# A decoder block on one core: the matmuls on zeros before the first products are left out

## The chip, the cores and the metric

The kernel runs on one core of a Trainium2 chip. The metric is the time of one execution on the device in microseconds (us). One execution was also recorded by the profiler; every row below comes from it, and its times count from the start of its span.

## The reference

One layer of a hybrid decoder on x (1 x 1024 x 1024, float32). Two parts, each with an RMSNorm before and after and a residual:

```python
h = rms_norm(x, norm_mix_pre)
proj = h @ w_in                       # 1024 x 1792
u_pool, g_b, g_c, u_conv, q, k, v = split(proj)
y_pool = pool_mixer(u_pool, pool_w, pool_scale)
y_conv = g_b * causal_dwconv(g_c * u_conv, conv_w)
y_attn = swa_sink_attention(q, k, v, attn_sinks)
x = x + rms_norm(concat(y_pool, y_conv, y_attn) @ w_o, norm_mix_post)
h = rms_norm(x, norm_ffn_pre)
up = causal_dwconv(h @ ffn_w_up, ffn_conv_w) + ffn_conv_b     # 1024 x 5632
x = x + rms_norm((silu(gate) * val) @ ffn_w_down, norm_ffn_post)
```

## The kernel before

The program is written by hand for each engine, in order, with semaphores between them. Rows of x are normalised in 8 tiles of 128 tokens, turned with TensorE transposes so that channels stand on the partitions, and multiplied by the weights. Each float32 operand is split into a rounded high part (ScalarE, into a float32r tile) and the low rest (VectorE), and a product is three matmuls: high by high, high by low, low by high (`product`, L1613 to L1619). After the projection come attention, pooling and convolution, the output projection, the up projection and the down projection, the last two partly with seven products in place of eight. TensorE works through all of it in the order in which its block of the program is written.

The change lies at the start of that block. What is before it on each engine:

- SyncE (L548 to L562) starts the loads in this order: x tiles 0 and 1, the identity matrix, the gain as 8 rows, weight tile 0, x tiles 2 and 3, and so on.
- GpSimd sets small constants (L642 to L644), among them `pool_mat`, a 128 x 256 tile of zeros that is later filled with the pooling weights; the semaphore `set_` counts these. Then it makes the mean square and its root for each tile (`root`, L645).
- ScalarE squares tiles 0 and 1 (`square_x`, L757), rounds weight tile 0 (L744), rounds turned tiles 0 and 1 into `hhi` (`round_h`, L768), and squares tiles 2 and 3.
- VectorE normalises tiles 0 and 1 (`norm_x`, L1126), copies the turned gain (L1161), multiplies the turned tiles 0 and 1 by it in PSUM (`scale_turned`, L1155), makes the low part of weight tile 0 (L1116) and of x tiles 0 and 1 (`low_h`, L1138), and then normalises tiles 2 and 3 (L1131).
- TensorE waits until the constants are set, runs 8 matmuls of `pool_mat` with itself into bank 0 of PSUM (`keep_clock(8)`), waits for the identity and the gain rows, turns the gain (L1684), turns x tiles 0 and 1 (`turn_x`, 8 transposes each, L1626), and runs 4 more matmuls on zeros (`keep_clock(4)`). Their result is read by nobody: the first product into the same bank starts its accumulation anew. A call of a 128 x 256 float32 matmul is two records in the trace.

Then the projection begins, by pairs of x tiles. For the first pair weight tiles 0 and 1 are multiplied in three passes of 8 matmuls each (`channels_by_pass`, L1645, matmuls at L1664) so that a pass can start when its operand is there. For weight tile 0 the passes are high by high (A), weight's low part (B), x's low part (C). In weight tile 1 the turn of x tile 2 stands before the first pass and that of tile 3 before the second. From the second pair on the three matmuls of a product follow each other (L1616 to L1618), and the turns of the tiles 4 to 7 come between the weight tiles.

Of the kernel before, what the change touches and what calls it, by code (L numbers as in the profile page):

```python
# [24 lines left out]
P = 128  # L25
# [55 lines left out]
def build(nc, consts, x, norm_mix_pre, w_in, pool_w, pool_scale, conv_w, attn_sinks, w_o,  # L81
# [18 lines left out]
    with ctx:  # L100
        def alloc(stack, name, shape, dt=F32):
            return stack.enter_context(nc.sbuf_tensor(name, shape, dt))
# [69 lines left out]
        pool_mat = alloc(xb_, "pool_mat", [P, 2, P])  # L172
# [55 lines left out]
        ps = ctx.enter_context(nc.psum_tensor("ps", [P, 8, HALF], F32))  # L228
# [1383 lines left out]
        def _(pe):  # L1612
# [17 lines left out]
            def turn_x(t):  # L1630
                if t >= 2:
                    pe.wait_ge(ht_split, t - 1)
                turn(t, hrow_a[:, t % 2, :])
# [37 lines left out]
            def project(m, n, c, ks=range(KD)):  # L1671
                return channels(use_banks(m) + c, n % SPLIT, hhi, hlo, half_of(c), ks)

            def keep_clock(n):

                for _ in range(n):
                    pe.matmul(ps[:, 0, 0:2 * P], pool_mat[:, 0, :], pool_mat[:, :, :],
                              start=True, stop=True)

            pe.wait_ge(set_, 3)  # L1680
            keep_clock(8)
            pe.wait_ge(ident_in, 16)
            pe.wait_ge(gain_rows_in, 16)
            pe.transpose(ps[:, 3, 0:KD], gain_rows[0:KD, :], ident[0:KD, 0:KD])              .then_inc(gain_turned, 1)  # L1684
            turn_x(0)
            turn_x(1)
            keep_clock(4)

            for pair in range(NT // 2):
                tiles = slice(2 * pair, 2 * pair + 2)  # L1690
# [104 lines left out]
            for u in range(SLOTS):  # L1795
                n, c = SLOT0 + u // 2, u % 2
# [202 lines left out]
```

## Time and profile before

| what | value |
| --- | --- |
| median of 3 runs | 950.22 us (950.14 to 950.29) |
| the profiled execution, its own time | 950.0 us |
| its span, first to last instruction | 948.2 us |
| TensorE busy, share of the span | 938.9 us, 99% |
| VectorE, ScalarE, GpSimd busy | 654.7, 433.5, 189.4 us |
| mean granted clock of TensorE | 0.999 |

Engines are PE (TensorE's matmuls), PEld (its weight loads, which overlap them), DVE (VectorE), ACT (ScalarE), POOL (GpSimd) and SP (SyncE). A transpose is a matmul of its line L1626. A record of a matmul is longer than the step to the next one, because matmuls are pipelined: the step is the rate, the record the latency. Where several instructions of one kind follow each other, a timeline prints one row with their count and the time from the first start to the last end.

### The profile page before, as it was taken

How to read it: one execution, taken by the hardware profiler on the slowest of the kernel's cores; microseconds unless marked ns; L12 is line 12 of the kernel's file. 1: busy time of each engine (PE TensorE's matmuls, PEld its weight loads, DVE VectorE, ACT ScalarE, POOL GpSimd, SP SyncE). 2: the span in 40 equal slices, each digit the busy share in tenths (PEclk: the TensorE clock that was granted, in tenths of full speed). 3: DMA queues.
4: the chain of work that ended last, by engine and by line, in shares of the span. 5: the costliest groups of instructions: out<-in, count | busy, mean ns of one | idle time of the engine just before them, and what ended most of it. 6: DMA issues, size and time to landing. Idle time of an engine off the chain costs nothing.

```text
span 948.2 us, 11487 instructions
## 1 busy us (share of the span) xinstructions
PE 938.9 (99%) x4419; PEld 777.9 (82%) x4419; DVE 654.7 (69%) x710; ACT 433.5 (46%) x648; POOL 189.4 (20%) x182
## 2 busy tenths in 40 slices
PE   8999999999999999999999999999999999999997
PEld 7988887887888888888888888888888888888886
DVE  6645795766655899777877787778776653535668
ACT  5524444444433555445443444444444454335353
POOL 3301000000111424242223333443431100000021
PEclk9999999999999999999999999999999999999999
DMA  6999971005322236486343446554647775677455
GB/s 225 269 328 231 209 145 45 23 23 178 134 89 89 90 97 206 142 184 183 115 141 100 145 112 133 112 143 105 140 91 208 201 235 214 228 267 264 163 171 200
DMA packets 114248, 151.16 MB, mean 159 GB/s; under 512 B 6289, under 2 KB 66193, under 8 KB 114193
## 3 DMA queue, kind: packets, MB, share of 16 engines
q1 hardware_dynamic: 100737, 118.63, 38.5%
q0 software_dynamic: 13456, 31.79, 16.8%
q8 instruction: 35, 0.57, 0.3%
q14 instruction: 20, 0.16, 0.1%
HBM read 113.17 MB, written 60.29 MB: 183 GB/s over the span
## 4 chain that ended last, share of the span: by engine, by line
PE 97%; DVE 1%; DMA 0%; ACT 0%; POOL 0%; issue 0%; DVEq 0%; POOLq 0%; SPq 0%; ACTq 0%
PE ps L1616 30%; PE ps L1618 30%; PE ps L1617 30%; PE ps L1626 1%; PE ps L1751 1%; PE ps L1774 1%; PE ps L1752 1%; PE ps L1760 1%; PE ps L1778 1%; DMA xin<-in_x 0%; DVE hlo L1138 0%; PE ps L1789 0%; DVE ps L1155 0%; PE ps L1664 0%; DVE x2b L1427 0%
## 5 line engine op out<-in xcount | busy, mean ns | idle before, releaser
L1616 PE MATMUL ps<-hhi,whi 128*128 128x512 f32 (+1 forms) x240 | 91.1, 379 | 0.5 <-DVE hlo L1138 0.5
L1618 PE MATMUL ps<-hhi,wlo 128*128 128x512 f32 (+1 forms) x240 | 88.5, 369 | 0.0
L1617 PE MATMUL ps<-hlo,whi 128*128 128x512 f32 (+1 forms) x240 | 88.5, 369 | 0.0
L686 POOL TENSOR_TENSOR w_sums<-wraw 128x1024 f32<-128x1024 f32 x20 | 48.4, 2421 | 185.8 <-DVE w2lo L1373 63.0
L648 POOL TENSOR_SCALAR meansq<-sumsq 128x1 f32<-128x1 f32 x28 | 10.0, 357 | 373.4 <-ACT yg L1042 170.8
L1616 PEld LDWEIGHTS ps<-hhi,whi 128*128 128x128 f32 x240 | 45.3, 189 | 8.0 <-DVE hlo L1138 0.7
L1001 ACT ACTIVATE yg<-ps,par_b 128x1024 f32<-128x1024 f32 x21 | 25.3, 1207 | 57.9 <-DVE ps L1499 57.9
L1618 PEld LDWEIGHTS ps<-hhi,wlo 128*128 128x128 f32 x240 | 45.2, 189 | 7.7
L1617 PEld LDWEIGHTS ps<-hlo,whi 128*128 128x128 f32 x240 | 45.3, 189 | 7.4 <-issue 0.5
L1447 DVE SCALAR_TENSOR_TENSOR yg<-ps,par_a,yg 128x1023 f32<-128x1023 f32 x22 | 28.2, 1282 | 26.9 <-ACT yg L1001 26.9
L1616 PE MATMUL ps<-h2hi,whi 128*128 128x512 f32 x116 | 45.4, 391 | 0.2 <-DVE wraw L1148 0.2
L1618 PE MATMUL ps<-h2hi,wlo 128*128 128x512 f32 x116 | 45.2, 389 | 0.0
L1617 PE MATMUL ps<-h2lo,whi 128*128 128x512 f32 x116 | 45.1, 389 | 0.0
L1461 DVE TENSOR_TENSOR w2lo<-wraw,w2hi 128x1024 fp32r<-128x1024 f32 x23 | 27.8, 1223 | 23.5 <-ACT w2hi L1031 23.1
L1616 PE MATMUL ps<-r_hi,whi 128*128 128x512 f32 x112 | 43.6, 389 | 0.0
L1618 PE MATMUL ps<-r_hi,wlo 128*128 128x512 f32 x112 | 43.6, 389 | 0.0
L1618 PE MATMUL ps<-r_hi,w2lo 128*128 128x512 f32 x112 | 43.6, 389 | 0.0
L1616 PE MATMUL ps<-r_hi,w2hi 128*128 128x512 f32 x112 | 43.6, 389 | 0.0
L1617 PE MATMUL ps<-r_lo,w2hi 128*128 128x512 f32 x112 | 43.6, 389 | 0.0
L1616 PE MATMUL ps<-r_hi,h2hi 128*128 128x512 f32 x112 | 43.6, 389 | 0.0
L1617 PE MATMUL ps<-r_lo,h2hi 128*128 128x512 f32 x112 | 43.6, 389 | 0.0
L1618 PE MATMUL ps<-r_hi,h2lo 128*128 128x512 f32 x112 | 43.6, 389 | 0.0
(261 smaller groups left out, 2709.1 us busy)
## 6 DMA issues: line engine op xcount, KB each, us to landing
wraw<-in_ffn_w_up SPq DMA_DIRECT2D x42, 512.0 KB, 5.2
s_dram<-in_ffn_w_down POOLq DMA_DIRECT2D x6, 2816.0 KB, 28.1
wraw<-r_dram SPq DMA_DIRECT2D x44, 256.0 KB, 3.7
wraw<-s_dram SPq DMA_DIRECT2D x44, 256.0 KB, 4.9
r_dram<-cst SPq DMA_DIRECT2D x33, 256.0 KB, 2.8
wraw<-act_dram SPq DMA_DIRECT2D x33, 256.0 KB, 3.6
wraw<-in_ffn_w_down SPq DMA_DIRECT2D x33, 256.0 KB, 4.6
wraw<-in_w_in SPq DMA_DIRECT2D x14, 512.0 KB, 10.2
```

Source lines behind the costliest of these rows:

```text
L648: pool.tensor_scalar(meansq[:, i:i + 1], sumsq[:, i:i + 1], 1.0 / DM, EPS, ALU.mult, ALU.add).then_inc(ms_ready, 1)
L686: pool.tensor_tensor(w_sums[:, 0:2, :], raw[:, 0:4:3, :], raw[:, 2:3, :].broadcast_to([P, 2, HALF]), ALU.add)\
L1001: act.activation(yg[:, pair % 2, :], banks(4 * (pair % 2)), ACT.Identity, bias=ffn_bias(pair), scale=ffn_tap(2, pair)).then_inc(yg_started, 1)
L1447: finish_step(dve.scalar_tensor_tensor(y[:, 1:], src[:, :SEQ - 1], ffn_tap(1, f), y[:, 1:], ALU.mult, ALU.add))
L1461: dve.tensor_tensor(lo, raw, hi, ALU.subtract).then_inc(d_split, 1)
L1616: pe.matmul(acc, w_hi, x_hi, start=first, stop=False, skip_group_check=looped)
L1617: pe.matmul(acc, w_hi, x_lo, start=False, stop=False, skip_group_check=looped)
L1618: return pe.matmul(acc, w_lo, x_hi, start=False, stop=last, skip_group_check=looped)
L1626: last = pe.transpose(ps[:, b + k // 4, (k % 4) * P:(k % 4 + 1) * P], rows[:, k * P:(k + 1) * P], ident)
L1751: pe.matmul(acc, q, k_hi[:, kv, keys], start=True, stop=False)
L1752: last = pe.matmul(acc, q, k_lo[:, kv, keys], start=False, stop=True)
L1760: last = pe.transpose(ps[:, 6, i * P:(i + 1) * P], s_sb[:, u % 2, i, :], ident)
```

## The change

The helper `keep_clock` and its two calls are taken out; nothing else differs.

```diff
-            def keep_clock(n):
-
-                for _ in range(n):
-                    pe.matmul(ps[:, 0, 0:2 * P], pool_mat[:, 0, :], pool_mat[:, :, :],
-                              start=True, stop=True)
-
             pe.wait_ge(set_, 3)
-            keep_clock(8)
             pe.wait_ge(ident_in, 16)
             pe.wait_ge(gain_rows_in, 16)
             pe.transpose(ps[:, 3, 0:KD], gain_rows[0:KD, :], ident[0:KD, 0:KD])              .then_inc(gain_turned, 1)
             turn_x(0)
             turn_x(1)
-            keep_clock(4)
```

## Rows read from the trace of the kernel before

**Rows 1.** The page: busy time of each engine; shares of the chain by engine.

```profile
PE 938.9 (99%) x4419; PEld 777.9 (82%) x4419; DVE 654.7 (69%) x710; ACT 433.5 (46%) x648; POOL 189.4 (20%) x182
...
PE 97%; DVE 1%; DMA 0%; ACT 0%; POOL 0%; issue 0%; DVEq 0%; POOLq 0%; SPq 0%; ACTq 0%
```

**Rows 2.** Busy by stretch (PE first, records started), then TensorE's waits after 60 us.

```profile
30.00:60.00 30.00, 30.00 (x190) 27.00 (x189) 17.20 (x18) 11.93 (x12) 7.12 (x13) 1.00 0.95 290
...
PE ps L1616 <- DVE wraw L1148: 0.2, 1, 0.2
```

**Rows 3.** Timeline of TensorE, 0 to 13 us: start, length, line, count, [idle before].

```profile
1.26 5.57 PE L1677 MATMUL ps<-pool_mat 128*128 128x256 f32 x16 [1.26 <-POOL pool_mat L644]
...
7.25 1.09 PE L1626 MATMUL ps<-cst,hrow_a 128*128 128x128 f32 x8 [0.27 <-DVE hrow_a L1126]
8.72 1.09 PE L1626 MATMUL ps<-cst,hrow_a 128*128 128x128 f32 x8 [0.38 <-DVE hrow_a L1126]
9.65 1.89 PE L1677 MATMUL ps<-pool_mat 128*128 128x256 f32 x8
12.24 0.98 PE L1664 MATMUL ps<-hhi,whi 128*128 128x256 f32 x6 [0.70 <-ACT hhi L768]
```

**Rows 4.** Line L1677 in four stretches: count, ns min/median/max, first and last start.

```profile
L1677 PEld LDWEIGHTS ps<-pool_mat x8: 287/337/337, 1.3 to 4.0; 128*128 128x128 f32 x8
L1677 PE MATMUL ps<-pool_mat x7: 634/634/794, 1.3 to 4.0; 128*128 128x256 f32 x7
...
L1677 PE MATMUL ps<-pool_mat x4: 380/558/634, 4.0 to 5.2; 128*128 128x256 f32 x4
...
L1677 PEld LDWEIGHTS ps<-pool_mat x8: 190/190/192, 9.5 to 10.9; 128*128 128x128 f32 x8
L1677 PE MATMUL ps<-pool_mat x8: 379/379/382, 9.6 to 11.2; 128*128 128x256 f32 x8
```

**Rows 5.** Line L1677 on PE by stretch: stretch, length, busy (records), granted clock, DMA.

```profile
1.26:4.40 3.14, 3.14 (x7) 1.00 0.84 284
```

**Rows 6.** The chain that ended last, 7.9 to 21.2 us: start, length, what.

```profile
7.91 0.49 DVE hrow_a L1126
...
8.77 2.36 DVE ps L1155 x2
...
12.26 2.28 DVE hlo L1138 x2
...
18.79 1.04 ACT hhi L768
...
21.14 0.39 PE ps L1616
```

**Rows 7.** Busy of the five engines in stretches at the end, then granted clock, DMA.

```profile
946.00:947.00 1.00, 0.00 (x0) 0.00 (x0) 0.00 (x0) 0.00 (x0) 0.00 (x0) 1.00 1.00 387
947.00:948.20 1.20, 0.00 (x0) 0.00 (x0) 0.00 (x0) 0.00 (x0) 0.00 (x0) 0.55 0.20 77
```

**Rows 8.** Lines L1626 and L1664: ns min/median/max, first and last start.

```profile
L1626 PE MATMUL ps<-cst,hrow_a x64: 272/273/330, 7.2 to 33.6; 128*128 128x128 f32 x64
...
L1664 PE MATMUL ps<-hhi,wlo x16: 279/283/283, 13.3 to 20.4; 128*128 128x256 f32 x16
```

**Rows 9.** Timeline of TensorE, 13 to 18 us.

```profile
13.29 1.12 PE L1664 MATMUL ps<-hhi,wlo 128*128 128x256 f32 x8
14.58 1.21 PE L1664 MATMUL ps<-hlo,whi 128*128 128x256 f32 x8 [0.17 <-DVE hlo L1138]
15.86 1.06 PE L1626 MATMUL ps<-cst,hrow_a 128*128 128x128 f32 x8
16.68 1.20 PE L1664 MATMUL ps<-hhi,whi 128*128 128x256 f32 x8
17.72 1.04 PE L1626 MATMUL ps<-cst,hrow_a 128*128 128x128 f32 x8
```

**Rows 10.** Timeline of VectorE, the normalising of tile 2.

```profile
14.44 1.27 DVE L1131 SCALAR_TENSOR_TENSOR hrow_a<-xin,rstd,gain_a 128x1024 f32<-128x1024 f32 x1
```

## The prediction

> **What bounds the kernel now.** I read the page's header parts first. TensorE is busy for 938.9 of 948.2 us, and of the chain that ended last 97% is TensorE [rows 1]. So a delay of TensorE reaches the end of the kernel unless a later wait swallows it. The second reading asks for such waits: from 30 to 60 us TensorE is busy for all 30.00 us, and after 60 us it waits once, for 0.2 us [rows 2]. There is no slack that could take up a delay. What is left is the first 21 us, where TensorE waits for others, and where the removed instructions lie.
>
> The timeline of TensorE there [rows 3] shows the first burst of matmuls on zeros from 1.26 to 6.83 us (8 calls, 16 records), the turn of the gain row, the turns of x tiles 0 and 1 at 7.25 and 8.72, the second burst from 9.65 to 11.54 (4 calls, 8 records), and the first useful product, pass A of weight tile 0, at 12.24. Neither burst holds anybody up: the turn at 7.25 waited for the normalised rows and pass A for the rounded ones; the table names VectorE and ScalarE as releasers.
>
> The rows that matter are those of the bursts themselves [rows 4]. A record that started up to 4.0 us takes 634 ns, its weight load 337 ns; from 5.2 us on and in the second burst it is 379 and 190 ns. The steps changed alike: seven starts in the 3.14 us from 1.26 give 0.449 us, while the second burst gives (1.89 - 0.379)/7 = 0.216 us, a factor of 2.08. [...] From the whole first burst: 5.57 - 0.38 = 5.19 us are 15 steps, n of them slow, n x 0.449 + (15 - n) x 0.216 = 5.19, so n = 8.4, and the change came 3.8 us after 1.26, at about 5.0 us; the mixed row from 4.0 to 5.2 fits. The granted-clock column prints 1.00 for 1.26 to 4.40 us all the same [rows 5], so I trust the durations and not that column.
>
> **What the change does.** It takes out 24 matmul records and adds no wait. Time taken off the path: none. Both bursts ended before what follows them could begin. The turn of the gain row may start earlier, since it stands behind the burst, but the copy that reads it stands on VectorE behind the normalising of tile 1, which the chain contains [rows 6]: worth 0.
>
> The second burst alone would also be worth about 0. It fills a pause that would last from 9.81 (end of the second turn) to 12.24, 2.4 us. At the end of the kernel TensorE issues its last product shortly before 942.6, and the granted clock is still 1.00 until 947.0 and 0.55 on average from there [rows 7], so it fell at about 947.1, after 4.5 us of idleness. A pause of 2.4 us should not lower it.
>
> The first burst is what counts. Without it TensorE does nothing for 6 us and starts the turns at the lower level. **Term 1, the turns.** Eight take 1.09 us now, with 0.273 us for one [rows 3, 8]: a step of (1.09 - 0.273)/7 = 0.117 us. No row shows a slow turn. The bounds on the factor are 337/190 = 1.77 (weight loads) and 2.08 (steps); I take 1.9, between them, since a turn is a short load and a short stream: 0.222 us. Tile 0 starts at 7.25 as now; tile 1 is in the queue behind it and starts at 7.25 + 8 x 0.222 = 9.03 (its rows are there at 8.66); its last turn starts at 10.58 and takes 0.273 x 634/379 = 0.46, so it ends at 11.04. VectorE now begins scaling tile 1 at 9.95, half-way through the pair of 2.36 us that starts at 8.77 [rows 6], held by its own queue and not by the turn. With a semaphore's 0.04 it begins at 11.08: **+1.13 us**. Tile 0's scaling (about 9.3 for 8.77) hides in that. All of the scaled path, rounding on ScalarE included, moves by 1.13, so pass A starts at 13.37.
>
> **Term 2, the passes.** Passes A and B of weight tile 0 are 16 matmuls. The step at full clock is (1.12 - 0.283)/7 = 0.12 us [rows 8, 9]; times 1.9 it is 0.228, and 16 of them last until 13.37 + 3.65 = 17.02. When does the clock rise? The only case in this trace is 3.8 us of unbroken work before the change; from 13.37 that is 17.17, just as pass C starts, of which one step stays slow (0.1 us). Pass C needs the low parts of x, ready at 14.54 + 1.13 = 15.67: no wait any more. C, turn 2, the first pass of weight tile 1 and then turn 3 follow: 8 x 0.12 + 0.10 = 1.06, then 0.82 and 1.04 (the differences of starts 15.86, 16.68, 17.72 [rows 9]): turn 3 starts at 19.94 in place of 17.72, **+2.2 us**. The two waits that TensorE has now in this stretch, 0.2 us before pass C and about 0.3 before turn 2 (its rows come at 14.44 + 1.27 = 15.71 [rows 10]), are swallowed. VectorE's rows for turns 2 and 3 come at 16.8 and 18.6, both earlier than TensorE gets there.
>
> From turn 3 on the chain is turn, rounding at 18.79, low part, first product of the next pair, 21.14 now [rows 6]: everything follows turn 3, so the lag of 2.2 stays, and there is no later slack.
>
> **Sum.** The traced execution took 950.0 us, span 948.2, and the median of the runs is 950.22. 950.0 + 2.2 = 952.2 for a profiled one, 952.4 against the median. With 1.77 for the factor the same working gives +1.8 (turns 0.9 of it); with 2.08, +2.6. A difference under 0.2%, 1.9 us, can't be told from none here, and the forecast stands a little beyond it.
>
> [...]
>
> **Rivals.**
> 1. *The turns themselves raise the clock.* Slow turns would run from 7.25 to 11.04 without a pause, 3.8 us, as long as the first burst needed. Then the pause to 13.37 (2.3 us, under the 4.5 of [rows 7]) keeps the clock up, passes run fast, and only term 1 is left: +1.1, 951.35, not slower by the bound. It decides if the rise comes before about 16.5 us, because each slow us of passes costs 0.47 us. For it: the near equality of the two times. Against it: the turns at 7.25 came when the clock was already up, so no row shows that turns raise it. [...] Chance 0.27, with rises inside passes A and B.
> 2. *The rise comes later than in the first burst.* 3.8 us is one observation. If pass C and turn 2 stay slow too, C ends at 17.02 + 1.82 = 18.84, turn 2 at 20.6, and turn 3 starts at 21.7: +3.9 to +4.0, 954.2; half-way there, 953.3. Nothing in the rows excludes it. Chance 0.25.
> 3. *The clock stays low up to the next pair.* TensorE turns between passes would break up the work. C, turn 2, pass, turn 3 and two more passes at 1.8 us each from 17.02 end at 27.9, where the pair's products start now at 21.14 (+6.7), and their first 3.8 us cost 1.8 more: +8.5, 958.7. Against it: A, B and C are 5.5 slow us without a turn between. Chance 0.04.
> 4. *Nothing happens*: the clock is full from the start, as the column says [rows 5]: 950.2. Against it: 634 for 379 ns. With it, a gain, for which I find no place. Chance 0.04.
>
> **The numbers.** The forecast has 0.40, at 952.4, its own range 952.0 to 952.8. The range reaches down to rival 1 with term 1 at factor 1.77 (950.22 + 0.9 = 951.1) and up to rival 2's end with 0.1 to spare (954.3); outside are rivals 3 and 4 and a few in a hundred beside. Slower by over 0.2% (above 952.1) are nearly all of the forecast, 0.35 of 0.40, and rivals 2 and 3: 0.64 in all, of which I keep 0.62. Within 0.2% are rival 1, the lowest forecasts and rival 4: 0.36. Faster 0.02.
>
> **What would show it.** In the changed trace: transposes of tiles 0 and 1 with longer records (about 0.46 us) and a step of 0.22; scaling of tile 1 near 11.1; pass A at 13.4 with records near 0.47 and a step of 0.23, falling to 0.283 and 0.12 near 17.2; turn 3 near 19.9 and the first product of pair 1 at 23.3; from there every start later by the same 2.2. Records of pass A at 0.283 mean rival 1; of pass C and turn 2 at the slow length, rival 2. The prediction is wrong if turns are fast from the beginning, or if the lag at 60 us isn't the lag at the end.

## The result, and the profile after

| | before | after |
| --- | --- | --- |
| median | 950.26 us | 952.15 us |
| lowest to highest, 16 runs each | 949.96 to 950.44 | 951.32 to 953.26 |
| the profiled execution, span | 950.0, 948.2 us | 951.97, 950.2 us |

The ratio is 1.0022, with an interval of 1.0015 to 1.0029: 1.9 us slower, where 2.2 had been forecast. The second row of the table is as telling as the first. The kernel before repeats within 0.5 us, the changed one spreads over 1.9 us, and its times gather near 952.0 (10 of 16 between 951.86 and 952.29) and near 953.1 (5 of 16 between 953.03 and 953.26); one is at 951.32. Beside the experiments below single times of the kernel before lie between 949.66 and 951.15, so only a spread well beyond that says something.

First the page of the changed kernel, for the rows that answer to [rows 1], then two of TensorE's waits (us in total, how often, the longest).

```profile
PE 934.0 (98%) x4395; PEld 775.0 (82%) x4395; DVE 654.9 (69%) x710; ACT 433.5 (46%) x648; POOL 189.6 (20%) x182
...
PE 97%; DVE 1%; ACT 1%; DMA 0%; POOL 0%; issue 0%; DVEq 0%; POOLq 0%; ACTq 0%
```

```profile
PE ps L1664 <- ACT hhi L768: 2.4, 1, 2.4
...
PE ps L1616 <- DVE wraw L1148: 0.2, 1, 0.2
```

24 records are gone, and TensorE is busy for 4.9 us less in a run that is 2 us longer. (Lines after the removed helper have moved; L1677 is here the turn of the gain row.) The last of these waits is the only one after 30 us, as in [rows 2]: no slack has appeared. The pause before pass A, where the second burst stood, is 2.4 us. The two short waits of [rows 3, 9] before pass C and turn 2 have gone.

The timeline of TensorE, against [rows 3, 9]:

```profile
6.23 0.24 PE L1677 MATMUL ps<-cst,gain_rows 8*128 8x8 f32 x1 [6.23 <-DMA cst<-consts_dram]
7.58 3.68 PE L1626 MATMUL ps<-cst,hrow_a 128*128 128x128 f32 x16 [1.11 <-DVE hrow_a L1126]
13.64 2.08 PE L1664 MATMUL ps<-hhi,whi 128*128 128x256 f32 x8 [2.38 <-ACT hhi L768]
15.52 1.56 PE L1664 MATMUL ps<-hhi,wlo 128*128 128x256 f32 x8
16.91 1.12 PE L1664 MATMUL ps<-hlo,whi 128*128 128x256 f32 x8
...
19.70 1.04 PE L1626 MATMUL ps<-cst,hrow_a 128*128 128x128 f32 x8
```

And the records of the two lines, by stretch, against [rows 8] (count, ns min/median/max):

```profile
L1626 PE MATMUL ps<-cst,hrow_a x16: 421/421/476, 7.6 to 10.8; 128*128 128x128 f32 x16
...
L1664 PE MATMUL ps<-hhi,whi x8: 415/415/580, 13.6 to 15.3; 128*128 128x256 f32 x8
...
L1664 PE MATMUL ps<-hlo,whi x8: 278/283/288, 16.9 to 17.7; 128*128 128x256 f32 x8
```

The turns (421 ns a record, 273 in [rows 8]) and pass A (415 ns) run at the lower level from end to end, pass B changes in its middle, pass C (283 ns) is at the higher one. As the first burst did [rows 4], TensorE's first work begins slow: here these are the turns, after 6.23 us with nothing to do, the 8 x 8 turn of the gain and a pause of 1.11. Steps: (3.68 - 0.42)/15 = 0.217 us for turns, and between the starts of A and B 1.88/8 = 0.235. B to C is 1.39 = n x 0.235 + (8 - n) x 0.12, where n is the number of steps still at the lower level; so n = 3.7, and the clock rose at 15.52 + 0.87 = 16.4 us.

The chain in this stretch, against [rows 6]:

```profile
7.58 3.69 PE ps L1626 x16
...
11.30 1.24 DVE ps L1155
...
12.56 1.03 ACT hhi L768
...
13.64 4.39 PE ps L1664 x24
```

Before, VectorE stood in this chain from 8.77 to 14.54, one operation behind the other, and TensorE only came in with pass C. Now the chain goes through both turns, once over VectorE and ScalarE, and then stays on TensorE. This is how a slower engine takes over a chain that it had not been on.

The column of the granted clock (the number after the five engines) shows nothing of the slow turns, as it showed nothing in [rows 5]:

```profile
7.00:11.20 4.20, 3.62 (x16) 3.28 (x16) 2.59 (x4) 1.40 (x3) 0.97 (x2) 1.00 0.95 300
```

So the 1.97 us by which this execution is behind the traced one of before are: 0.33 because its first turn began at 7.58 and not at 7.25 (the rows of x came later: VectorE began on them at 6.77 us, 6.44 before; nothing in the edit touches these loads, and in all 14 traces, with and without the bursts, it begins between 6.19 and 6.84); 1.07 for the turns (pass A begins 6.06 us after the first turn, before 4.99); 0.58 for the passes (turn 3 begins 6.06 us after pass A, before 5.48). Against the median of before, 950.26, this execution is 1.7 us behind: the traced one of before was itself a short one.

### The profile page after: what moved, and what is told of

It is laid out like the page before. It is cut to its first block, busy times and chain, and to the rows that moved or that the text cites. A ratio compares the mean times of both kernels' runs of the same rounds, so it can differ in the third digit from the quotient of the medians.

```text
span 950.2 us, 11439 instructions
## 1 busy us (share of the span) xinstructions
PE 934.0 (98%) x4395; PEld 775.0 (82%) x4395; DVE 654.9 (69%) x710; ACT 433.5 (46%) x648; POOL 189.6 (20%) x182
## 4 chain that ended last, share of the span: by engine, by line
PE 97%; DVE 1%; ACT 1%; DMA 0%; POOL 0%; issue 0%; DVEq 0%; POOLq 0%; ACTq 0%
PE ps L1616 30%; PE ps L1618 30%; PE ps L1617 30%; PE ps L1626 2%; PE ps L1743 1%; PE ps L1766 1%; PE ps L1744 1%; PE ps L1752 1%; PE ps L1770 1%; PE ps L1664 1%; DMA xin<-in_x 0%; PE ps L1781 0%; ACT hhi L768 0%; DVE x2b L1427 0%; DVE ps L1155 0%; DVE hlo L1138 0%
## 5 line engine op out<-in xcount | busy, mean ns | idle before, releaser
L1617 PE MATMUL ps<-r_lo,whi 128*128 128x512 f32 x112 | 43.6, 389 | 0.0
```

Source lines behind the costliest of these rows:

```text
L1617: pe.matmul(acc, w_hi, x_lo, start=False, stop=False, skip_group_check=looped)
```

## The experiments

Three questions stood open. Is the loss made of the two terms? Do turns raise the clock? And what is each burst worth? The medians below are of 11 runs each. Every edit shown below is against the kernel before.

| run | median, lowest to highest | ratio to before, interval |
| --- | --- | --- |
| again (the changed kernel) | 952.04, 951.12 to 953.18 | 1.0018, 1.0009 to 1.0027 |
| fill_matmuls | 951.22, 951.08 to 951.55 | 1.0010, 1.0001 to 1.0019 |
| fill_turns | 951.28, 950.94 to 951.37 | 1.0010, 1.0002 to 1.0019 |
| second_only | 951.25, 951.19 to 951.40 | 1.0011, 1.0002 to 1.0019 |
| first_only | 951.02, 950.29 to 952.30 | 1.0009, 1.0001 to 1.0018 |
| first_six | 950.90, 950.07 to 952.06 | 1.0006, 0.9997 to 1.0015 |
| first_half | 951.90, 951.25 to 952.77 | 1.0018, 1.0010 to 1.0027 |
| late_start | 951.55, 951.17 to 951.79 | 1.0013, 1.0004 to 1.0021 |
| second_1 | 950.26, 950.09 to 951.26 | 1.0003, 0.9994 to 1.0012 |
| second_2 | 950.21, 949.91 to 951.19 | 1.0001, 0.9992 to 1.0010 |

The kernel before had 950.22, 950.27 and 950.25 beside them.

### The changed kernel again

No edit in any of the three.

> The changed kernel once more, beside the experiments of this call, to see whether its time and the moment at which the clock rises repeat. My theory (the start at the lower clock costs about 1.1 us in the turns of x tiles 0 and 1 and about 0.9 us in the passes of weight tile 0, and all of it reaches the end): median 952.0 to 952.5. In the first profile the records of pass B shortened at about 16.4 us, 2.8 us after pass A began. Rival A (the moment is always the same distance behind the work): again 2.8 us, single times within 0.3 us of each other. Rival B (the moment moves from execution to execution): another distance here, and single times spread over more than 1 us, as they did (951.3 to 953.3).

> A third look at the changed kernel, to see which moments of the clock come with which time. Two looks so far: rise at 16.4 us (951.97), and rise at 9.9, fall at 13.7, rise at 17.1 (951.4). Theory (the loss is 0.45 to 0.5 us for each slow us in which passes or turns on the chain run, whatever the moments): the sum from this look's own records agrees with its time within 0.3 us. For a time near 953.2 the rise should come at 18.5 us or later.

> A fourth look at the changed kernel, for the same reading as the third: the start of turn 3 behind that of the kernel before, against the time behind 950.2, should agree within 0.3 us, and slow records in passes A to C or in turn 2 should account for all of it beyond 1.0 us.

The first had 11 runs, the other two one execution each (953.83 and 953.02 us). In the profile of the first (951.40 us) the timeline of TensorE reads:

```profile
6.99 3.43 PE L1626 MATMUL ps<-cst,hrow_a 128*128 128x128 f32 x16 [0.60 <-DVE hrow_a L1126]
12.80 1.57 PE L1664 MATMUL ps<-hhi,whi 128*128 128x256 f32 x8 [2.38 <-ACT hhi L768]
14.17 1.91 PE L1664 MATMUL ps<-hhi,wlo 128*128 128x256 f32 x8
```

and its busy time by stretch (stretch, length, busy time and records, granted clock, then what the DMA moved):

```profile
12.80:13.60 0.80, 0.80 (x6) 0.91 1.18 357
13.60:16.40 2.80, 2.80 (x15) 0.50 0.46 172
16.40:17.40 1.00, 1.00 (x9) 0.77 0.01 4
```

The last turns are already fast (3.43 in place of 3.68), pass A starts fast, and then the clock falls. A mean of 0.91 over 0.8 us, where the column prints 0.50 while the clock is down, means half the clock for 0.14 us of it, so the fall was at 13.46, with TensorE at work for 0.7 us after its pause of 2.4; 0.77 over 1 us puts the rise at 16.86. In the other two every turn of tiles 0 and 1 is at the lower level (3.68 us). In again_c (953.02 us) it is low to the beginning of turn 2:

```profile
13.47 2.07 PE L1664 MATMUL ps<-hhi,whi 128*128 128x256 f32 x8 [2.38 <-ACT hhi L768]
15.34 1.91 PE L1664 MATMUL ps<-hhi,wlo 128*128 128x256 f32 x8
17.05 1.91 PE L1664 MATMUL ps<-hlo,whi 128*128 128x256 f32 x8
18.75 1.23 PE L1626 MATMUL ps<-cst,hrow_a 128*128 128x128 f32 x8
```

Three passes of 1.91 us, and a turn that is slow in its first part (1.23 for 1.03). again_b has the same picture and 953.83 us, 0.8 more, which lies in its first turn: it began at 8.22, because the gain row, which stands before it in TensorE's queue, landed only at 8.0. Rival B holds: the same work behind the same pause sees the clock rise at 16.4, at 9.9 with a fall at 13.46, or in the course of turn 2, at about 19 (again_c) and 20 (again_b). Behind the start of pass A that is 2.8, 5.7 and 5.8 us where it had not risen before.

Both expectations on the sum hold as well. The start of turn 3 and the execution's own time, each behind the traced execution of before (17.72 and 950.0):

| profile | first turn | pass A | turn 3 | behind at turn 3 | own time | behind at the end |
| --- | --- | --- | --- | --- | --- | --- |
| before | 7.25 | 12.24 | 17.72 | | 950.00 | |
| changed | 7.58 | 13.64 | 19.70 | 1.98 | 951.97 | 1.97 |
| again | 6.99 | 12.80 | 19.09 | 1.37 | 951.40 | 1.40 |
| again_b | 8.22 | 14.28 | 21.62 | 3.90 | 953.83 | 3.83 |
| again_c | 7.41 | 13.47 | 20.77 | 3.05 | 953.02 | 3.02 |
| fill_matmuls | 7.53 | 13.58 | 19.05 | 1.33 | 951.37 | 1.37 |
| fill_turns | 7.45 | 13.50 | 18.98 | 1.26 | 951.29 | 1.29 |
| first_only | 7.58 | 12.46 | 18.76 | 1.04 | 951.02 | 1.02 |
| late_start | 7.65 | 14.61 | 19.50 | 1.78 | 951.73 | 1.73 |
| first_half | 7.34 | 13.16 | 20.24 | 2.52 | 952.50 | 2.50 |
| second_only | 7.34 | 13.40 | 18.88 | 1.16 | 951.19 | 1.19 |
| first_six | 7.62 | 12.62 | 18.93 | 1.21 | 951.17 | 1.17 |
| second_1 | 7.96 | 12.65 | 18.96 | 1.24 | 951.26 | 1.26 |
| second_2 | 7.53 | 12.53 | 18.14 | 0.42 | 950.43 | 0.43 |

Nothing after turn 3 takes up or adds more than 0.07 us, in any of these 14 profiles.

### The two terms apart: the pause filled

```diff
-            keep_clock(8)
...
-            keep_clock(4)
+            keep_clock(2)
```

> No first burst; 2 calls on zeros (4 records) after the turns of x tiles 0 and 1, which fill the pause before pass A: 4 x 0.449 = 1.8 us from about 11.0, so they end before pass A at 13.4. The turns stay at the lower clock: +1.1 stays. My theory (unbroken work raises the clock, and here it is unbroken from 7.3 us on): the clock rises before pass A or early in it, and term 2 is gone: 951.3 to 951.6. Rival (only the work of pass A and after it counts, or the moment is a matter of chance): as the changed kernel, 952.2.

```diff
-            keep_clock(8)
...
-            keep_clock(4)
+            for _ in range(9):
+                pe.transpose(ps[:, 0, 0:P], pool_mat[:, 0, :], ident)
```

> As the run with 2 calls on zeros, but the pause is filled with 9 turns of zeros (9 x 0.222 = 2.0 us), so that TensorE does nothing but transposes from 7.3 to about 13.3 us. If turns raise the clock as matmuls do: records shorten before or early in pass A, 951.3 to 951.6, like the run with matmuls. [...]

```diff
-            keep_clock(8)
...
             keep_clock(4)
```

> No first burst, the second of 4 calls (8 records) stays. After slow turns that end at about 11 us, 8 records at the lower clock take 8 x 0.449 = 3.6 us, so the burst, if the clock doesn't rise in it, ends at about 14.5 and holds pass A back by 1.1 us. My theory: the clock rises within or at the end of the burst, the passes run fast, pass A starts between 13.4 and 14.5, waits before pass C and turn 2 take up some of it: 951.4 to 952.1. Rival (the clock rises no sooner than in the changed kernel): pass A late and slow, 953.

All three give 951.2 to 951.3, and all 33 times lie between 950.94 and 951.55. In each, pass A begins 6.05 or 6.06 us after the first turn, as in the changed kernel, and turn 3 5.47 or 5.48 us after pass A, as in the kernel before. That is term 1 alone, measured: +1.0 us (1.06 from first turn to pass A in the profiles). The rivals, 952.2 for fill_matmuls and 953 for second_only, are out; the two fills came a shade under the 951.3 to 951.6 expected. Term 2 is the rest, 952.1 - 951.25 = 0.9 us on average, and it is what spreads. second_only came out below the 951.4 to 952.1 expected, because the clock rose within its 8 records: the burst took 2.77 us and didn't hold pass A back.

The timeline of fill_turns, and below it the records of its 9 added turns and of the matmuls that follow:

```profile
7.45 3.68 PE L1626 MATMUL ps<-cst,hrow_a 128*128 128x128 f32 x16 [1.14 <-DVE hrow_a L1126]
10.91 2.13 PE L1687 MATMUL ps<-cst,pool_mat 128*128 128x128 f32 x9
13.50 1.21 PE L1664 MATMUL ps<-hhi,whi 128*128 128x256 f32 x8 [0.46 <-ACT hhi L768]
```

```profile
L1687 PE MATMUL ps<-cst,pool_mat x9: 421/421/421, 10.9 to 12.6; 128*128 128x128 f32 x9
...
L1664 PE MATMUL ps<-hhi,whi x8: 278/282/387, 13.5 to 14.4; 128*128 128x256 f32 x8
```

TensorE did nothing but transposes from 7.45 to 13.04, all of them at the lower level, and the matmuls after them run at the higher one (the longest, 387 ns, is the first after a pause: in the changed kernel that one took 580). So turns do raise the clock. In the profile of again, too, the records of turns shortened at about 9.9 us with only turns (and the 8 x 8 turn of the gain) before them.

### What the second burst is worth

```diff
             keep_clock(8)
...
-            keep_clock(4)
```

> The first burst of 8 calls back in, the second burst of 4 left out. My theory: the pause between the turns and pass A is 2.4 us, too short to lower the clock, so the second burst is worth nothing: 950.2 +- 0.2, turns with records of 0.273 us, pass A at about 12.24 with records of 0.283. Rival (the second burst holds the clock through the pause): pass A and part of B at records of 0.415 us, turn 3 about 1 us later, 951.2.

I was wrong here. The rival holds in its numbers, though the fall came within pass A and not ahead of it. The median is 0.8 us above the kernel before and single times spread over 2 us, from 950.29 to 952.30. The timeline:

```profile
1.26 6.24 PE L1677 MATMUL ps<-pool_mat 128*128 128x256 f32 x16 [1.26 <-POOL pool_mat L644]
...
12.46 1.48 PE L1664 MATMUL ps<-hhi,whi 128*128 128x256 f32 x8 [2.44 <-ACT hhi L768]
13.74 1.91 PE L1664 MATMUL ps<-hhi,wlo 128*128 128x256 f32 x8
15.45 1.65 PE L1664 MATMUL ps<-hlo,whi 128*128 128x256 f32 x8
```

and its stretches:

```profile
12.40:13.60 1.20, 1.14 (x8) 0.84 1.08 328
13.60:16.20 2.60, 2.60 (x14) 0.50 0.72 255
16.20:17.20 1.00, 1.00 (x9) 0.78 0.53 90
```

The clock was up for the turns (records of 273 ns), TensorE paused for 2.44 us, pass A began at full clock, and at 12.40 + 0.82 = 13.22 the clock fell and stayed down to 16.64. Pass A's first records alone would show nothing: the price of the pause came 0.8 us after it had ended, under dense work. That the pause brings it on rests on comparison: with 4 records put into it (second_2, fill_matmuls), 8 (the kernel before, second_only) or 9 turns (fill_turns) no profile has such a fall.

Two runs with a shorter pause, `keep_clock(4)` replaced by 2 calls and by 1:

> The kernel before with 2 calls in place of 4 in the second burst: TensorE stands still for about 1.6 us before pass A (0.7 in the kernel before, 2.4 without the burst). Without the burst single times spread from 950.3 to 952.3, and the profile showed the clock falling 1 us after pass A began. Theory P (a pause of 2.4 us can lower the clock, depending on where it falls; the second burst is there for that): something between, a median of 950.2 to 950.6, with a few times near 951. Rival (only the end of the first burst matters, the pause doesn't): as without the second burst, 951.0 with times up to 952.3.

> The same with 1 call: a pause of about 2.0 us. Theory P: median 950.3 to 951.0, spread of the single times nearer to 2 us. Rival: 951.0 with times up to 952.3, as without the burst.

Medians of 950.21 and 950.26, which can't be told from before. The spread hints at an effect that the medians hide. With 1 call (a pause of 2.2 us) 4 of 11 times are above 951.0; with 2 calls (1.6 us) one, at 951.19, and another at 950.89. Of the kernel before, 3 of 87 runs beside these experiments are above 951.0, but 2 of those are among the 21 that ran beside these two. Theory P fits, and is shown only weakly by these times; that 2 calls are worse than 4 isn't shown, and the median of 1 call is just below the 950.3 to 951.0 that it expected. The profile of second_1, 951.26 us, is one of its slow four:

```profile
12.65 1.21 PE L1664 MATMUL ps<-hhi,whi 128*128 128x256 f32 x8 [2.19 <-ACT hhi L768]
13.70 1.68 PE L1664 MATMUL ps<-hhi,wlo 128*128 128x256 f32 x8
```

```profile
13.60:14.60 1.00, 1.00 (x9) 0.70 1.15 373
```

Again fast at first (1.21 us for pass A), slow later. By its granted clock (0.70 over 1 us, so half the clock for 0.6) the fall came at 14.0, 1.35 us after pass A began. From pass A to turn 3 this execution needs 6.31 us, 0.83 more than before.

### What the length of the first burst is worth

The second burst left out in both, the first of 6 and of 4 calls.

> A first burst of 6 calls (12 records), no second burst: to about 5.8 us if the clock rises at 5.0. Theory 1 (the burst need only last until the clock rises): 950.2 with single times within 0.3 us. If the moment of the rise moves from execution to execution by more than a microsecond: most times at 950.2, some at 952.

> A first burst of 4 calls in place of 8, no second burst: 8 records from 1.26 to about 4.9 us, all at the lower clock, then nothing until the gain is turned at 6.2. In the kernel before the rise came at about 5.0 us. Theory 1 (the work done by then is enough, the clock rises shortly after): turns at 0.273 us records, 950.2. Theory 2 (it has to be at work when the clock rises, or longer): turns at 0.421, like the changed kernel, 952.2. If the moment moves from execution to execution, single times spread over both.

6 calls behave as 8 do without the second burst (950.90, with an interval that still holds 1, against 951.02). In their profile all 12 records of the burst are at the lower level, and the 8 turns that begin 0.9 us after its end take 1.10 us, as at full clock:

```profile
L1677 PE MATMUL ps<-pool_mat x12: 633/635/797, 1.3 to 6.1; 128*128 128x256 f32 x12
```

```profile
7.62 1.10 PE L1626 MATMUL ps<-cst,hrow_a 128*128 128x128 f32 x8 [0.67 <-DVE hrow_a L1126]
```

So the clock rose in the 0.9 us between, in which TensorE did nothing but the 8 x 8 turn of the gain. It fell again at 13.9, in pass B. 4 calls give 951.90, most of the loss, though the profile has tile 0's turns at full clock for the most part:

```profile
1.26 3.68 PE L1677 MATMUL ps<-pool_mat 128*128 128x256 f32 x8 [1.26 <-POOL pool_mat L644]
6.11 0.20 PE L1684 MATMUL ps<-cst,gain_rows 8*128 8x8 f32 x1 [1.17 <-DMA gain_rows<-in_norm_mix_pre]
7.34 1.28 PE L1626 MATMUL ps<-cst,hrow_a 128*128 128x128 f32 x8 [1.04 <-DVE hrow_a L1126]
8.81 1.97 PE L1626 MATMUL ps<-cst,hrow_a 128*128 128x128 f32 x8 [0.19 <-DVE hrow_a L1126]
```

Granted clock by stretch, same columns as above:

```profile
8.00:9.00 1.00, 0.81 (x5) 0.56 0.80 194
9.00:17.80 8.80, 6.42 (x29) 0.50 0.74 235
```

It fell at about 8.1 us, behind two pauses of 1.2 and 1.0 us with one 8 x 8 turn between, and was low until 18.4. Neither theory of the expectation is quite it: the burst did raise the clock, and it was lost again after the pauses. That the pauses did it is argued from this one profile; no run fills them behind 4 calls. Single times from 951.25 to 952.77 cover both.

### A delay alone

```diff
-            keep_clock(4)
+            keep_clock(11)
```

> The kernel before with 11 calls in place of 4 in the second burst: the clock is up throughout, and only the start of pass A is pushed back, to 9.65 + 22 x 0.216 = 14.4 us in place of 12.24 (+2.2). It measures by itself how a delay at this place reaches the end. My theory: the two waits in the passes (0.2 before pass C, 0.3 before turn 2) take up some 0.5 us, turn 3 comes 1.6 to 1.8 us later, and all of that reaches the end: 951.9. Rival (slack later takes it up): 950.2 to 951. Rival (no cover at all): 952.4.

951.55 in place of 951.9. Here the clock is up and only the place of pass A changes.

```profile
10.05 4.91 PE L1677 MATMUL ps<-pool_mat 128*128 128x256 f32 x22
14.61 1.31 PE L1664 MATMUL ps<-hhi,whi 128*128 128x256 f32 x8
...
19.50 1.04 PE L1626 MATMUL ps<-cst,hrow_a 128*128 128x128 f32 x8
```

Turn 3 comes 4.89 us after pass A, 5.48 before: the two short waits take up 0.59 us, where I had said some 0.5. From one record to the next it is 4.56/22 = 0.207 us, not 0.216, which makes the delay 0.2 us smaller than planned; and the profiled execution had its rows of x 0.4 us later than that of before (VectorE normalises tile 1 at 8.31 us, 7.91 before), which is no part of the edit. What is left of the delay reaches the end, 1.78 at turn 3 and 1.73 in time.

## Why the prediction was right, step by step

- **No slack, everything reaches the end**: right. The lag at turn 3 and the lag at the end agree within 0.07 us in all 14 profiles.
- **Nothing comes off the path**: right, the gain's turn moved to 6.23 and nobody began earlier.
- **Term 1, turns, +1.13**: right in mechanism, and measured at +1.0 to +1.07 where all turns are slow; in again, where the last ones are fast, it is 5.81 - 4.99 = 0.82. The turns do start slow without the first burst: 421 ns a record in the changed kernel and 273 in the kernel before. The step is 0.217 (0.222 forecast), so the factor that no row had shown is 0.217/0.117 = 1.85 (1.9 taken), and the last record takes 0.421 (0.46). The 0.04 from the end of the last turn to the scaling is there as well: 7.58 + 3.68 = 11.26 us, and VectorE begins at 11.30 (11.08 forecast).
- **Term 2, passes, +1.1**: near the 0.9 measured, and in part by luck. The step of 0.228 at the lower level was a good estimate (1.91 us for 8 are (1.91 - 0.415)/7 = 0.214, and 0.235 in pass A, whose longest record takes 0.580). But the prediction took 3.8 us of unbroken work as the delay of the clock, from one observation. The rise came at 16.4, 9.9, 19 and 20 us in four executions of the same program, and 17.2 was forecast. Term 2 is then 0.58 us (changed), 0.81 (again), 1.86 (again_b) and 1.82 (again_c), each as turn 3 less pass A against 5.48. The forecast's +1.1 is none of these four; it lies between two kinds of execution. The single times have a group at 952.0 and one at 953.1, the changed profile (951.97) is of the first and again_c (953.02) of the second. The mean of the 16 times is 952.4, which is the forecast, while the median, 952.15, lies in the first group. That every time of a group has its profile's moments isn't shown. In the traced execution the sum came out near for another reason still: 0.33 us of its 1.97 are the later first turn, and the passes cost half of what was forecast.
- **"A pause of 2.4 us should not lower it"**, and with it "the second burst alone would also be worth about 0": wrong. This step failed outright. With only the second burst left out the kernel takes 951.02, and where the clock fell the profiles show it 0.7 to 1.4 us after the pause. I had taken 4.5 us of idleness at the end of the kernel as the price of a fall. That was one fall behind complete stillness, and it doesn't bound what a shorter pause does. It cost the forecast little, since the second burst was removed together with the first.
- **Rival 1**: its first half is true, turns raise the clock, in fill_turns and in one of four profiles of the changed kernel. Its second half isn't: in that profile the clock so won was lost again behind the pause. That may be why no execution of the changed kernel has come below 951.1. Its number, 951.35, is met by fill_turns, 951.28.
- **Rival 2**: the two slower profiles. Its full end needs turn 2 slow throughout, and the clock was up from the middle of it: 1.82 and 1.86 us for term 2. again_b is 3.83 behind all the same, because 0.97 of it is its late first turn.
- **Rival 3** and **rival 4** weren't seen. For rival 4 the column of the granted clock had spoken. It prints 1.00 in the changed kernel's first slow stretch too (turns of 421 ns), and 0.50 only after a fall. In these traces it shows changes from the first fall on, not the level at the start: it is 1.00 all through the slow passes of again_b (14.20 to 19.50 us) and again_c (13.40 to 18.70) too.
- **The waits in this stretch are swallowed**: right. Slow work in the first profile was 3.7 us of turns and 2.8 of passes. By the measured steps, 0.217 for 0.117 in turns and 0.235 for 0.12 in passes, an estimate of what that takes more is 1.7 + 1.4 = 3.1 us, against the 1.65 of terms 1 and 2 there. About half of it did not reach the end: TensorE had been waiting in this stretch before, 0.4 us for tile 1's rows and 0.6 in the passes.

Not forecast was that the first turn's own start moves between 6.99 and 8.22 us over the four profiles, with the landing of x and of the gain row; it is part of the spread of single times.

## What to carry to other kernels

In this kernel TensorE is the bound and has to wait for its first data (VectorE ends tile 0's rows between 6.9 and 7.6 us over the 14 traces). Matmuls on zeros in that time cost 0.2 us in the one execution that shows a cost (second_1). With the next pause filled too they were worth 1.9 us: 1.0 for the first work and 0.9 for what follows. Keep such a filler going up to that work (4 calls in place of 8, with the pause left open, gave back little: 951.90, against 952.15 without any), but not past the moment at which its data are there (late_start: 1.3 us lost). Fill the next pause as well, for what such a pause costs showed only 0.7 to 1.4 us into the work after it. Judge such a filler by the spread of single times and not by the median alone. Price a slow stretch by the chain: only the part of it that no other engine's work covers reaches the end, here 1.65 of an estimated 3.1 us.

## What the runs showed of the hardware that I had not expected

- The clock can fall while TensorE is densely at work, 0.7 to 1.4 us after a pause of 2.2 to 2.4 us (13.46 us in again, 13.22 in first_only, 13.9 in first_six, 14.0 in second_1). In again it stayed down to 16.86, in first_only to 16.64. It can also rise where TensorE does next to nothing: in first_six between 6.8 and 7.6 us.
- Transposes alone bring the clock up (fill_turns, 5.6 us of turns before it was up).
- The moment of the change isn't a property of the program. In the same first burst of 8 calls the change came at 5.0 us in the kernel before, and the burst took 5.57 us; in first_only it took 6.24 us, in second_2 5.20 and in second_1 6.62. By the same two steps as in the prediction (0.449 and 0.216 us) these last two put the rise at 4.3 and 7.0 us. Such a burst can be in the way a little: tile 0's rows were ready at 6.64 + 0.76 = 7.40 us, the gain's turn could start only at 7.43, and the first turn came at 7.58. In second_1, with rows ready at 7.40 too, it came at 7.96, and pass A at 12.65 for 12.46, so 0.2 us of that execution's 1.26 are the first burst's own doing.
